# The prompt's trunk ahead of the sample's, its expert rows gathered beside it, and mixed rounds of 3 gather and 5 dense tiles

## What is computed

```python
x = layer_norm(x, ln_in_g, ln_in_b)
h = x @ w_in
o = diff_attention(q, k, v, lam, alibi_slopes())
o = head_rms_norm(o, subln_g, 1.0 - linit).reshape(B, S, ATTN_WIDTH)
f = fourier_mix(xf, w_fourier, b_fourier).reshape(B, S, FOURIER_WIDTH)
mix = jnp.concatenate([o, f], axis=-1) @ w_out
x = layer_norm(DEEPNORM_ALPHA * x + mix, ln1_g, ln1_b)
x = layer_norm(DEEPNORM_ALPHA * x + peer(x, peer_wq, peer_subkeys, peer_u, peer_v), ln2_g, ln2_b)
```

## Time and profile before

| what | us |
|---|---|
| median of 3 runs | 3909.4 |
| lowest and highest run | 3908.34 and 3912.4 |
| profiled execution, its own time | 3912.65 |
| its span | 3910.8 |
| busy in the span: PE | 3423.8 |
| DVE | 2943.6 |
| POOL | 1616.8 |
| ACT | 1100.2 |

### The profile page before, as it was taken

How to read it: one execution, slowest core, us unless ns; L and a number is a source line. 1 busy time by engine, 2 the same in 40 slices (tenths; PEclk the granted TensorE clock), 3 DMA queues, 4 the chain that set the end, 5 groups by cost and what they waited for, 6 DMA issues and landing times.

```text
span 3910.8 us, 49320 instructions
## 1 busy us (share of the span) xinstructions
PE 3423.8 (88%) x16412; PEld 2742.8 (70%) x16452; DVE 2943.6 (75%) x5233; ACT 1100.2 (28%) x1921; POOL 1616.8 (41%) x1473
## 2 busy tenths in 40 slices
PE   6999988899716777699999999999999999999995
PEld 3544455448615655688888888888888888888884
DVE  4000066326797764599999999999999999999999
ACT  1001266201107999422221222222222122221220
POOL 0000000000205878566555565555666555665551
PEclk9999999999858999899999999999999999999997
DMA  3011000110002555899998899898999998999994
GB/s 110 25 44 53 24 5 1 43 31 18 0 0 60 121 125 128 284 332 328 329 318 317 314 333 321 319 325 315 320 319 331 321 321 315 329 330 320 321 330 143
DMA packets 430103, 813.82 MB, mean 208 GB/s; under 512 B 221328, under 2 KB 239120, under 8 KB 429968
## 3 DMA queue, kind: packets, MB, share of 16 engines
q0 software_dynamic: 147456, 536.94, 37.9%
q1 hardware_dynamic: 282512, 275.35, 22.7%
HBM read 756.62 MB, written 55.57 MB: 208 GB/s over the span
## 4 chain that ended last, share of the span: by engine, by line
DVE 25%; PE 16%; issue 11%; DMA 6%; ACT 3%; DVEq 0%; POOL 0%; ACTq 0%; SPq 0%; POOLq 0%
PE twin L1055 8%; PE twin L1038 7%; DVE wbuf L1360 6%; DVE xln L1436 4%; DMA gate_sb<-spread_gates 4%; DVE xln L1371 3%; DVE peer_sb L1371 3%; DVE gate_sb L1394 2%; DVE al_sb L1398 2%; ACT uh_sb L557 1%; DVE vl_sb L1192 1%; DMA wbuf<-in_pv,gb 1%; DVE ul_sb L1192 1%; DVE peer_sb L1360 1%; DMA spread_gates<-big 1%
## 5 line engine op out<-in xcount | busy, mean ns | idle before, releaser
L517 POOL DMA_INDIRECT wbuf<-in_pu,idx_sb x384 | 498.1, 1297 | 334.7 <-DVE gate_sb L1360 233.0
L517 POOL DMA_INDIRECT wbuf<-in_pv,gb x384 | 441.0, 1149 | 417.3 <-DVE peer_sb L1371 169.0
L1055 PE MATMUL twin<-vh_sb,ah_sb 128*128 128x512 f32 x1536 | 493.6, 403 | 89.4 <-DVE xln L1436 80.4
L1038 PE MATMUL twin<-xh_sb,uh_sb 128*128 128x384 f32 x2048 | 521.3, 335 | 23.8 <-DVE ul_sb L1192 23.8
L1038 PE MATMUL twin<-xl_sb,uh_sb 128*128 128x384 f32 x2048 | 521.8, 335 | 0.0
L1038 PE MATMUL twin<-xh_sb,ul_sb 128*128 128x384 f32 x2048 | 521.3, 335 | 0.0
L1055 PE MATMUL twin<-vl_sb,ah_sb 128*128 128x512 f32 x1536 | 477.7, 392 | 0.0
L1360 DVE CUSTOM_DVE_ANT_0 wbuf<-wbuf,peer_sb 128x1024 f32<-128x1024 f32 x384 | 459.2, 1220 | 23.9 <-DMA wbuf<-in_pu,idx_sb 19.2
L1055 PE MATMUL twin<-vh_sb,al_sb 128*128 128x512 f32 x1536 | 476.3, 391 | 0.0
L1436 DVE TENSOR_TENSOR xln<-xln,twin 128x1024 f32<-128x1024 f32 x384 | 466.8, 1216 | 4.9 <-PE twin L1055 1.1
L1055 PEld LDWEIGHTS twin<-vh_sb,ah_sb 128*128 128x128 f32 x1536 | 277.7, 189 | 194.6 <-DVE xln L1436 143.1
(11 more groups left out here) (178 smaller groups left out, 5120.7 us busy)
## 6 DMA issues: line engine op xcount, KB each, us to landing
wbuf<-in_ut SPq DMA_DIRECT2D x128, 512.0 KB, 7.1
wbuf<-in_pv SPq DMA_DIRECT2D x128, 512.0 KB, 6.7
gate_sb<-spread_gates SPq DMA_DIRECT2D x128, 384.0 KB, 6.5
spread_gates<-wbuf SPq DMA_DIRECT2D x6, 4096.0 KB, 20.8
spread_gates<-big SPq DMA_DIRECT2D x6, 4096.0 KB, 20.8
wbuf<-in_dft_sample SPq DMA_DIRECT2D x4, 2048.0 KB, 8.1
wbuf<-in_pu,idx_sb POOLq DMA_INDIRECT x384, 7.3
wbuf<-in_pv,gb POOLq DMA_INDIRECT x384, 6.9
```

Of the source, the lines that this page charges most:

```text
L517: pool.indirect_dma_start(ring[s[0] % RING], None, (pu, pv)[v], bass.IndirectOffsetOnAxis(ap=(idx_u, idx_v)[v][:, slot:slot + 1], axis=0))\
L1038: last = nc.tensor.matmul(act_psum[e][:, h, 0:HN], lhs[:, e, k, :], rhs[:, k, h * HN:(h + 1) * HN], start=(k == 0 and rhs is xh and lhs is ...
L1055: last = nc.tensor.matmul(wide[t % 2][:, 512 * h:512 * h + 512], lhs[:, par, e, toks], rhs[:, e, 512 * h:512 * h + 512], start=(e == 0 and ...
```

## The change

The prompt's two tiles now go through the whole trunk first, with buffers of their own for the constants and the weights of that pass, and their picks are made at once. Then the sample's eight tiles go through the trunk. Beside them, DVE and POOL work off the prompt's 512 slots with a ring of four buffers (RING_P; two in big and two in qk): 240 slots ahead of the sample's attention, two in each of 30 of its 32 attention units (the other two take the activation function and the coefficients), four ahead of each of the 16 half tiles of the output projection, and the 148 that are left behind the second norm. The sample's tiles 2, 3 and 4 are gathered in the mixed rounds, tiles 5 to 9 are dense. The 64 rounds are written out one by one with 11 to 13 slots each, 12 on average, and DVE_ORDER has new places; "*" stands for the slots that are left over in the round, 3 to 5. PE's, ACT's and SP's parts of the trunk are ordered by request in the same way. POOL no longer copies the indices of a gather tile.

```diff
-BATCHES = [(2, S_SAMPLE // P), (0, S_PROMPT // P)]
+BATCHES = [(0, S_PROMPT // P), (S_PROMPT // P, S_SAMPLE // P)]
+NT_P = S_PROMPT // P
 DIST_W = 2 * S_SAMPLE - P
 RING = 8
-NG = 4
+NG_P, NG_S = 2, 3
+NG = NG_P + NG_S
+RING_P = 4
+FILL_BEFORE, FILL_UNIT, FILL_HALF = 240, 2, 4
+ACTS_AT_UNIT = 8
+assert FILL_BEFORE + ACTS_AT_UNIT * FILL_UNIT == NG_P * 128
...
+HALF_AT = [(2 * h * NP // (2 * NG_S) + 1) // 2 for h in range(2 * NG_S + 1)]
...
-DVE_ORDER = "1 v0 1 v1 5 g0 2 l0 2 u0 g1 a u1 1 a l1 1 a 1 a 1 a 1 a"
+DVE_ORDER = "1 v0 1 v1 * g0 1 l0 1 u0 g1 a u1 1 a l1 1 a 1 a 1 a"
...
+        ring_p = [big[:, 0:D], big[:, D:2 * D], qk[:, 0:D], qk[:, D:2 * D]]
...
+        def slots_of(q):
+
+            h = max(k for k in range(2 * NG_S) if HALF_AT[k] <= q)
+            rounds, j = HALF_AT[h + 1] - HALF_AT[h], q - HALF_AT[h]
+            return range(h * NSLOT + NSLOT * j // rounds, h * NSLOT + NSLOT * (j + 1) // rounds)
...
+            for n in range(2 * NG_P * NSLOT):
+                v, t, c = n // (NG_P * NSLOT), n // NSLOT % NG_P, n % NSLOT
+                if n == FILL_BEFORE:
+                    pool.wait_ge(dft_mm, 3 * 2 * HF)
+                    distances_of(1)
+                if v == 0 and c == 0:
+                    pool.wait_ge(retrieved, t + 1)
+                    pool.sem_inc(slots_free, 1)
+                if n == 2:
+                    pool.wait_ge(sc_ev, 4 * NT_P)
+                    pool.sem_inc(slots_free, 1)
+                if n >= RING_P:
+                    pool.wait_ge(row_used_p[n % RING_P], n // RING_P)
+                    pool.sem_inc(slots_free, 1)
+                pool.indirect_dma_start(ring_p[n % RING_P], None, (pu, pv)[v],
+                                        bass.IndirectOffsetOnAxis(ap=idx[:, t, c:c + 1], axis=0))\
+                    .then_inc(row_in_p[n % RING_P], 16)
...
+            def fill(count):
+                for n in range(filled[0], min(filled[0] + count, 2 * NG_P * NSLOT)):
+                    k, v, t, c = n % RING_P, n // (NG_P * NSLOT), n // NSLOT % NG_P, n % NSLOT
+                    dve.wait_ge(row_in_p[k], 16 * (n // RING_P + 1))
+                    y = xn[:, t, :]
+                    if v == 0:
+                        nc.vector.tensor_tensor_reduce(ring_p[k], ring_p[k], y, 1.0, 0.0, ALU.mult, ALU.add,
+                                                       act_p[:, t, c:c + 1]).then_inc(row_used_p[k], 1)
+                    else:
+                        acc = (y, sum_p)[c % 2]
+                        if c >= 2:
+                            dve.wait_ge(row_used_p[(n - 2) % RING_P], (n - 2) // RING_P + 1)
+                        if c == 1:
+                            nc.vector.tensor_scalar(acc, ring_p[k], coef_p[:, t, c:c + 1], None, ALU.mult)\
+                                .then_inc(row_used_p[k], 1)
+                        else:
+                            nc.vector.scalar_tensor_tensor(out=acc, in0=ring_p[k], scalar=coef_p[:, t, c:c + 1],
+                                                           in1=acc, op0=ALU.mult, op1=ALU.add)\
+                                .then_inc(row_used_p[k], 1)
+                        if c == NSLOT - 1:
+                            for m in (n - 1, n):
+                                dve.wait_ge(row_used_p[m % RING_P], m // RING_P + 1)
+                            nc.vector.tensor_tensor(y, y, sum_p, ALU.add).then_inc(merged_p, 1)
+                            dve.wait_ge(merged_p, t + 1)
+                    filled[0] += 1
...
+            def fill_unit(u):
+                if u == ACTS_AT_UNIT:
+                    prompt_acts()
+                elif u == ACTS_AT_UNIT + 1:
+                    prompt_coefs()
+                else:
+                    fill(FILL_UNIT)
+            norm_in(0, 0, NT_P)
+            norm_in(1, NT_P, NT)
...
+            attend(0, lambda u: None)
+            add_mix(0, lambda n: None)
...
-            with dve.Fori(0, NG) as t:
+            for t in range(NT_P):
+                for piece in retrieval(t, True):
+                    piece()
+                restart()
+            fill(FILL_BEFORE)
+            attend(1, fill_unit)
+            add_mix(1, lambda n: fill(FILL_HALF))
+            fill(2 * NG_P * NSLOT)
+            dve.wait_ge(iota_done, 5)
+            for t in range(NT_P, NG):
...
+                order, todo = DVE_ORDER.split(), list(slots_of(q))
+                single = sum(what == "1" for what in order)
+                t = 0
+                for what in order:
+                    if what[0] == "g":
+                        gated_part(q, int(what[1]))
+                    elif what[0] == "u":
+                        if q < NP - 1:
+                            weight_lo(0, q * 2 + 2 + int(what[1]), int(what[1]))
+                    elif what[0] == "v":
+                        if q:
+                            weight_lo(1, q * 2 + (int(what[1]) - 2), int(what[1]))
+                    elif what[0] == "l":
+                        lo_part(q, int(what[1]))
+                    elif what == "a":
+                        if q:
+                            add(q, t)
+                        t += 1
+                    else:
+                        for _ in range(1 if what == "1" else len(slots_of(q)) - single):
+                            slot(todo.pop(0))
...
-            tile(0, True, False)
-            with dve.Fori(1, NG - 1) as g:
-                tile(g, False, False)
-            tile(NG - 1, False, True)
+            for q in range(NP):
+                peer_round(q)
```

More of the change, by code:

```diff
@@ L174, in build @@
         rrms = sm(NT * H)
-        n_small[0] = n_mark
         mx8 = sm(PH)
@@ L331, in _ @@
+            load_consts(0)
+            for k in range(2):
+                sp.dma_start(dft_p[:, k], dft_prompt[k].rearrange("(c p) s -> p c s", p=P)).then_inc(dft_in[k], 16)
             for a, v in enumerate((lq1, lk1, lq2, lk2)):
@@ new lines, in take_std, with take_xt @@
+            def take_std(which, t0, t1):
+                act_e.wait_ge(var_done, which + 1)
+                nc.scalar.activation(std[:, t0:t1], veps[:, t0:t1], ACT.Sqrt).then_inc(std_done, 1)
+            def take_xt(b):
+                t0, nt = BATCHES[b]
+                for n in range(2 * t0, 2 * (t0 + nt)):
+                    t, half = divmod(n, 2)
+                    act_e.wait_ge(xt_mm, n + 1)
+                    evac(xtb[b][:, 4 * half:4 * half + 4, (t - t0) * P:(t - t0 + 1) * P],
+                         bank(n % 8).rearrange("p (c t) -> p c t", c=4)).then_inc(xt_ev, 1)
@@ new lines, in take_qk, with take_vf @@
+            def take_qk(b, m, a, w, n):
+                act_e.wait_ge(qk_mm, n + 1)
+                evac(qkb[b][:, m, a:a + w], bank(n % 4)[:, 0:w], scale=DQK ** -0.5 if m < 4 else 1.0)\
+                    .then_inc(qk_ev, 1)
+            def take_vf(b):
+                t0, nt = BATCHES[b]
+                n = 2 * t0
+                for m in range(2):
+                    for t in range(t0, t0 + nt):
+                        act_e.wait_ge(vf_mm, n + 1)
+                        evac(vf[:, t, 512 * m:512 * m + 512], bank(n % 8)).then_inc(vf_ev, 1)
+                        n += 1
@@ L871, in scores, with att_scores @@
+            def att_scores(u, first):
+                h, b, qt = units[u]
+                w_all = BATCHES[b][1] * P
                 for c in range(2):
-                    if u:
+                    if not first:
                         pe.wait_ge(biased, 2 * (u - 1) + c + 1)
                     rows = slice(c * DQK, (c + 1) * DQK)
-                    for k in range(0, nt * P, 512):
-                        w = min(512, nt * P - k)
-                        last = nc.tensor.matmul(wide[c][:, k:k + w], qkv[rows, h, q0:q0 + P],
-                                                qkv[rows, 4 + h, k0 + k:k0 + k + w], start=True, stop=True)
+                    for k in range(0, w_all, 512):
+                        w = min(512, w_all - k)
+                        last = nc.tensor.matmul(wide[c][:, k:k + w], qkb[b][rows, h, qt * P:(qt + 1) * P],
+                                                qkb[b][rows, 4 + h, k:k + w], start=True, stop=True)
@@ new lines, in add_mix @@
+            def add_mix(of, between):
+                t0, nt = BATCHES[of]
+                for n in range(2 * t0, 2 * (t0 + nt)):
+                    t, half = divmod(n, 2)
+                    between(n - 2 * t0)
+                    dve.wait_ge(wo_mm, n + 1)
+                    r = xn[:, t, 512 * half:512 * half + 512]
+                    nc.vector.scalar_tensor_tensor(out=r, in0=r, scalar=ALPHA, in1=bank(n % 8),
+                                                   op0=ALU.mult, op1=ALU.add).then_inc(wo_add, 1)
+                    dve.wait_ge(wo_add, n + 1)
+                    if half:
+                        ln_stats(t)
+                ln_apply(2 + of, t0, t0 + nt, x1_done, 1, 32 * (of + 1))
@@ L1304, in gates_b @@
                     step(nc.vector.reciprocal(gsum, gsum))
```

(15 more changed lines are left out.)

945 lines of the change are left out of this document (489 added, 456 removed).

## The result

The changed kernel takes 4005.9 us (median of 4 runs, 4003.8 to 4012.1) against 3910.7 for the kernel before in the same session: a ratio of 1.0248 with a 95% interval of 1.0234 to 1.0261. It is slower by 95 us. The forecast of 3969 lay 58 above the kernel before: the sign and the range were right, the size was short by 37. The profiled execution has 4012.11, its span is 4010.3.

A forecast was written before the change was run, and what follows sets the result against it. DVE was taken to bound the mixed rounds, PE 2 behind. Trunk, retrievals, slot stretches, attention, output projection, gates, hand-over, rounds and tail summed to 3970, with 1.85 around it 3972, at the median 3969 against 3912.65; range 3865 to 4060.

The forecast's parts named there:

- L: The 64 mixed rounds: 27.2 of DVE work, 2.0 waiting for the gate load, 0.9 other waits; 30.1 each, 1936 in all.
- Rival 1: Mixed rounds: the gate load lands near 4.5, the wait is 0.6, a round 28.7, time 3879; chance 0.13.
- rival 4: Rounds: PE's 320-column matmuls cost like 384's, round 31.0, time 4027; or fill landing 5.6, slot 1.94, 4031; chance 0.12.
- rival 3: Fill: rows land near 3, slot 1.25, time 3811, chance 0.03; the last paragraph gives this number to PE-bound rounds.
- C: The prompt's 240 slots before the sample's attention: 1.78 each plus 6 for the first row, 433.
- H: The 148 slots left, in front of the sample's retrievals: 1.78 each, less rows already fetched, 260.
- F: Output projection's 16 half tiles with four slots each: 7.15 per half tile, 114.
- D to G: Sample's attention 220, output projection 114, with 20 ahead of it and 23 behind, up to the sample's norm.
- Rivals 2 and 3: Fill rows faster: landing 4.2, slot 1.58, time 3892, chance 0.10; or landing near 3, slot 1.25, 3811, chance 0.03.
- Picks and the prompt's trunk: Retrievals: 112 for the prompt's two, 215 for the sample's four; the prompt's trunk ahead of them: 218.
- The trunk hides behind the fill: Before the sample's attention: PE's 353 of sample work runs beside DVE's slots, leaving PE idle some 190 of 545.
- The sign: Whole kernel slower, chance 0.67: rounds give back 295, gates 67; the prompt's slots cost 433 + 260 + about 30.

## Why the prediction was right in its sign, and short in its size

- **The rounds (L) were right in mechanism and size.** DVE's work was 27.3 for 27.2; the wait at the second gate part was forecast at 2.0 a round from a landing between 5.4 and 6.5 over a cover of 3.9, and is 130.2/64 = 2.03, from a landing of 5.95 in the mean over a cover of 4.0. That it hit to a hundredth is luck: the bounds came from a row that mixes two loads, and 2.0 was a choice between them. Moving the cover back took 106 us off, taking it away from the kernel before put 137 on. Rival 1, a load that lands near 4.5, is dead: of the 64 loads that count, with a median of 6.2, nine landed in under 5.0. In rival 4 (called rival 3 in the prediction's last paragraph) DVE would wait for PE; its adds waited 1.4 us for PE in the whole run, and PE's work was 1821.2/64 = 28.5 a round, not 30.2. For the order of a ring (the Trainium skill, "DMA: Bandwidth & Descriptors", section "Queues, rings and completion order") the prediction had put a landing near 6.5 and a wait of 2.6. The traces fit an order: in none of the change, the kernel before and the two kernels with moved slots did a gate load land ahead of an SP load that was issued before it. But the order is not what holds the load near that level: in the kernel before with the short cover every earlier load of SP had landed when the gate load for the second part was issued, 1.9 ahead in the median, and it still took 6.5.
- **The fill (C, H, and F with it) was right in mechanism and mis-sized.** The step that failed is the one that put a slot at 1.78: "I take 4.95" for the landing, and a turn that had no term for POOL's queue. Measured in the mean are 5.94 for the landing in C (of which 0.39 by the rows that met SP's loads) and 5.56 in H, and 1.09 and 1.05 for the way from the release to POOL's issue, where 0.81 stood. The turn is 8.2 in C in place of 7.1, a slot 2.05. That is +60 in C, +32 in H and, as a half tile with its four slots then takes 8.35 on average (first to last half tile, 125.3 over 15) in place of 7.15, +19 for the 16 half tiles, which is the +17 in D to G. The landing was taken from two stretches that hold two and four rows, with 1.5 and 1.25 other rows under way at an issue, where in C it is 2.3; the same line's median over 2000 to 3500 is 6.9. The runs with three and five buffers show that the landing rises with the rows under way, so a tight ring must be priced from the loaded end. The bound 5.1 of the own range was too low; the clause of rival 4 on a landing of 5.6 was closer.
- **Rivals 2 and 3, rows at their fastest, did not come.** No stretch of the fill had a median near 4.2. The estimate of 3.2 from the Trainium skill ("DMA: Bandwidth & Descriptors", section "Anatomy of one DMA — SWDGE (gpsimd) path") is below the shortest of the fill's rows, 4.0. The other rows under way are not the whole difference: the eight rows of the fill that were issued with nothing else under way, and no load of SP beside them, took 4.2 to 6.8, in the median 4.4.
- **Picks and the prompt's trunk were put too high, by 62 in all with the gates and the hand-over.** A pick costs 94.8/2 = 47.4 or 191/4 = 47.8, not 55: the 278.3 of the earlier trace rows held 36 of waits for ACT, most of them for the exponentials of the picks' gates, and the sample's picks in the change have 1.2 of waits in all.

  ```profile
  DVE small L1303 <- ACT small L657: 29.8, 2, 15.5
  DVE big L1207 <- ACTq L652: 24.5, 3, 17.9
  ```

  (Of the second row 17.9 lie ahead of the stage.) These savings, and 8 in the rounds, are why an error of 109 in the fill stretches shows as 40 in the sum. They have nothing to do with the fill, so that the time came out inside the forecast's own range is luck.
- **"The trunk hides behind the fill" was right.** In the change PE waits 228.7 for DVE's first attention unit, where some 190 of idle time were forecast, and in the kernel without slots it was ready for the sample's attention at 571, 227 us before DVE was in the change.

  ```profile
  PE twin L977 <- DVE small L1265: 228.7, 1, 228.7
  ```

- **The sign** rested on the prompt's slots and trunk costing more where they now stand than the rounds and the gates give back, and held: those gave back 303 and 73 (295 and 67 were forecast), and what stands ahead of the gates grew by 478. The range, 3865 to 4060, held the 4006; the forecast's own range of 3925 to 4010 just did.

## What to carry to other kernels

Work moved beside another stage is hidden only if that stage leaves its engine idle for long enough and its inputs come as fast as the engine takes them: price a ring as a row's whole turn over its buffers, with the landing under that load, and set it against the other engine's remaining time. Where one buffer is refilled between two reads, the instructions between them are its cover; count them again whenever the order, the width or the number of tiles changes. And put late inputs beside work that needs none: the same slots cost 2.0 us in a block of their own and 1.25 between attention's instructions.
